# One head's masked scores added before the last matmul, an output tile and weights prepared in freed columns, and the second layer's input laid out by token block

## What is computed

```python
# layer 0: hx = rmsnorm(x) * (1 + scale) + shift
(k_f, lf_f), (k_b, lf_b), v = _hgrn2_gates(h, w_in, lb)
q, z = jnp.split(h @ w_in[:, 3 * HGRN_WIDTH:], 2, axis=-1)
# gla_forward, once forward and once on reversed tokens
o_inter = jnp.einsum('bhnck,bhnkv->bhncv', q_c * jnp.exp(b_c), s_prev)
a = jnp.einsum('bhnck,bhnsk->bhncs', q_c * jnp.exp(b_c - b_mid), k_c * jnp.exp(b_mid - b_c))
a = jnp.where(tril, a, 0.0)
o_intra = jnp.einsum('bhncs,bhnsv->bhncv', a, v_c)
# o = o_f + o_b, rmsnorm per head, times silu(z), times w_out, gated residual
# layer 1: x = x + gate * ((y.astype(h.dtype) * silu(z)) @ w_out), with
u, z = jnp.split(h @ w_in, 2, axis=-1)
pooled = centred means of u over windows 2, 4, 8, 16 of a 64-token row, minus u
y = jnp.einsum('brwgi,gio->brwgo', pooled, w_grp) * scale
# then a final rmsnorm
```

## Time and profile before

| what | value |
|---|---|
| three timed executions, median | 2196.77 us |
| lowest, highest | 2195.98, 2197.83 us |
| the profiled execution's own time | 2198.93 us |
| its span, first to last instruction | 2197.1 us |
| mean granted TensorE clock | 0.985 |
| busy: TensorE, VectorE, ScalarE, GpSimd | 96%, 58%, 42%, 22% |

### The profile page before, as it was taken

The page is one execution under the profiler, slowest core; times in us unless marked ns, Lnnn a source line. Parts: engine busy times, 40 slices in busy tenths (PEclk is TensorE's granted clock), DMA queues, the critical chain, the costliest instruction groups (busy, mean ns, idle before and its releaser), DMA issues.

```text
span 2197.1 us, 30841 instructions
## 1 busy us (share of the span) xinstructions
PE 2111.0 (96%) x11810; PEld 1526.6 (69%) x11810; DVE 1284.9 (58%) x2328; ACT 930.7 (42%) x1968; POOL 475.5 (22%) x441
## 2 busy tenths in 40 slices
PE   5899999999999999999999999899999999998998
PEld 2667767777777777777777777677666666665665
DVE  7847547547557547557457457655553536465444
ACT  5745345345355355355255355444423131214222
POOL 2021222222222322322313212000151312100110
PEclk8899999999999999999999999899999999999999
DMA  6210110110110110210110110534221110203443
GB/s 273 91 53 11 45 53 11 51 47 11 58 39 11 58 39 11 63 34 11 63 35 14 59 34 21 182 125 144 97 71 51 39 63 19 86 10 134 150 148 114
DMA packets 106746, 144.36 MB, mean 66 GB/s; under 512 B 7136, under 2 KB 74224, under 8 KB 105584
## 3 DMA queue, kind: packets, MB, share of 16 engines
q1 hardware_dynamic: 99648, 125.72, 17.6%
q10 hardware_dynamic: 6960, 16.80, 2.0%
HBM read 108.91 MB, written 33.57 MB: 65 GB/s over the span
## 4 chain that ended last, share of the span: by engine, by line
PE 83%; ACT 6%; DVE 6%; issue 2%; DMA 1%; SPq 0%; DVEq 0%; ACTq 0%
PE bank L1253 22%; PE bank L1254 22%; PE bank L1258 21%; PE bank L1408 3%; PE bank L1393 3%; PE bank L1388 3%; PE bank L1419 3%; PE bank L1508 3%; PE bank L1372 1%; DVE xa L1036 1%; ACT kp L713 1%; DMA ada_sb<-in_ada_w 1%; DVE lacc L1095 1%; ACT junk L385 1%; PE bank L1350 1%
## 5 line engine op out<-in xcount | busy, mean ns | idle before, releaser
L1253 PE MATMUL bank<-h_hi,w_hi 128*128 128x512 f32 (+1 forms) x1472 | 576.7, 397 | 0.0
L1254 PE MATMUL bank<-h_hi,w_lo 128*128 128x512 f32 (+1 forms) x1472 | 549.6, 378 | 0.0
L1258 PE MATMUL bank<-h_lo,w_bf 128*128 128x512 bf16 (+1 forms) x1472 | 328.6, 366 | 0.0
L1253 PEld LDWEIGHTS bank<-h_hi,w_hi 128*128 128x128 f32 x1472 | 278.9, 189 | 55.5
L1254 PEld LDWEIGHTS bank<-h_hi,w_lo 128*128 128x128 f32 x1472 | 279.1, 190 | 47.5
L1258 PEld LDWEIGHTS bank<-h_lo,w_bf 128*128 128x128 bf16 x1472 | 133.7, 98 | 142.7 <-issue 25.2
L1253 PE MATMUL bank<-wo_hi,og_hi 128*128 128x512 f32 x512 | 207.3, 405 | 11.9 <-DVE wo_lo L1128 7.8
L1066 DVE SCALAR_TENSOR_TENSOR w_st<-w_st,cv,bank 128x128 f32<-128x128 f32 x560 | 193.6, 346 | 30.0 <-PE bank L1408 6.2
L1254 PE MATMUL bank<-wo_hi,og_lo 128*128 128x512 f32 x512 | 202.2, 395 | 0.0
L578 POOL TENSOR_TENSOR q<-qp,cv 128x512 f32<-128x512 f32 x64 | 78.8, 1231 | 541.0 <-PE bank L1393 273.4
L553 POOL TENSOR_TENSOR w_hi<-w_raw,zero_col 128x512 fp32r<-128x512 f32 x80 | 91.9, 1149 | 425.9 <-PE bank L1258 224.3
(11 more groups left out here) (168 smaller groups left out, 3533.8 us busy)
## 6 DMA issues: line engine op xcount, KB each, us to landing
w_raw<-in_w_in SPq DMA_DIRECT2D x80, 256.0 KB, 2.7
ada_sb<-in_ada_w SPq DMA_DIRECT2D x8, 1024.0 KB, 13.7
xt<-in_x SPq DMA_DIRECT2D x16, 512.0 KB, 6.0
ada_a<-in_ada_late SPq DMA_DIRECT2D x64, 128.0 KB, 2.0
ada_b<-in_ada_late SPq DMA_DIRECT2D x64, 128.0 KB, 2.1
gated_scratch<-o_t ACTq DMA_DIRECT2D x32, 256.0 KB, 2.4
og<-gated_scratch SPq DMA_DIRECT2D x16, 512.0 KB, 4.1
xr<-in_x SPq DMA_DIRECT2D x16, 512.0 KB, 4.9
```

The lines of the kernel that those rows point to most:

```text
L1253: pe.matmul(out_ap, hi, m_hi, start=start, stop=False)
L1254: pe.matmul(out_ap, lo, m_hi, start=False, stop=False)
L1258: return pe.matmul(out_ap, bf, m_lo, start=False, stop=stop)
```

## The change

1. **Masked scores added.** The forward masked scores of all four blocks are kept; the backward ones go into one tile `am_b`. VectorE adds the two (`asum`, 128x512), in iterations 18 to 21 ahead of the chain, and TensorE multiplies `asum` with v once, in the backward iterations. The forward iterations keep only the product with the states. GpSimd clears one tile more.
2. **Late modulation.** Its buffers move into the columns of `k_tok`. In the first head its pieces come in iterations 5 to 9 (3, 3, 3, 3 and 4), and the closing matmuls in 9 and 10; in the other heads the pieces stay and the matmuls move from 8 and 12 to 7 and 10. Two copies of `k_tok` on ScalarE wait for them.
3. **First output tile.** It is loaded right after the output weights, into input columns that the heads have done with, rounded on ScalarE and VectorE within iteration 22 of the last head. GpSimd, not ScalarE, cuts the high parts of the eight weight slices. The wide part of the tile waits for high parts alone (`wo_cut`), the bf16 part for the rests. The last transpose of the heads follows the first tile's product.
4. **Layer 1's input by token blocks.** `h1_hi` and `h1_lo` get a block index ahead of the k index. The first projection of layer 1 comes before the transposes of the last tile.
5. **Group loop.** It is written out, and the first projection of a group waits like all others.
6. **Last weights.** The raw second half is loaded once block slot 0 has been used for the last time; slices 0 to 3 are rounded, and slices 0 and 1 get their rests, in iterations 14 and 15 of the last group, with the first tile.

```diff
-def late_index(st, first, top):
-
-    i = 2 * (st - (4 if first else 1)) - (1 if top else 0)
-    return i if 0 <= i < NLATE else None
+def late_pieces(st, first, top):
+
+    if first:
+        n = 4 if st == 9 else 3
+        seen = range(3 * (st - 5), 3 * (st - 5) + n) if 5 <= st <= 9 else range(0)
+        return seen[:1] if top else seen[1:]
+    i = 2 * (st - 1) - (1 if top else 0)
+    return range(i, i + 1) if 0 <= i < NLATE else range(0)
...
-    return {11: 0, 14: 1}.get(st) if first else {8: 0, 12: 1}.get(st)
+    return {9: 0, 10: 1}.get(st) if first else {7: 0, 10: 1}.get(st)
...
+                if g == 3 and n == NBLK:
+                    sp.wait_ge(s["proj_done"], HEADS * NG + 61)
+                    for j in range(2, 4):
+                        sp.dma_start(wo_raw1b[:, 2 * j - 4:2 * j - 2, :],
...
+            load_gated(sp, 0, 0)
             sp.wait_ge(s["x_done"], NX * HEADS)
-            load_gated(sp, 0, 0)
...
+            pool.wait_ge(s["proj_done"], HEADS * NG)
+            pool.wait_ge(s["gate_out"], 16)
+            for k in range(KT):
+                pool.wait_ge(s[f"wo_in{k // 2}"], 16)
+                pool.tensor_copy(wo_hi0[:, k, :], wo_raw0[:, k, :]).then_inc(s["wo_cut"], 1)
             round_gated(0)
...
+                    if last and st == NG - 1:
+                        round_tile(0, 0)
...
+                    if last and st == NG - 1:
+                        rest_tile(0, 0)
...
                     fi = st - (F0 + 3)
+                    if 6 <= fi < NF:
+                        ai = lat(fi)
+                        need(dve, "a_masked", NA, h, ai + 1)
+                        need(dve, "o_done", NA, h, ai)
+                        dve.tensor_tensor(asum[:, :, :], am[:, GROUPS[F0 + fi][1], :, :], am_b[:, :, :], ALU.add
+                                          ).then_inc(s["a_summed"], 1)
...
-            rest_weights(0, range(3))
-            rest_tile(0, 0)
-            rest_weights(0, range(3, KT))
+            rest_weights(0, range(KT))
+            rest_tile(0, 1)
             gate_out(HEADS, -1)
...
+                    if g == 3 and st == 14:
+                        rest_weights(1, range(1))
+                    if g == 3 and st == 15:
+                        rest_weights(1, range(1, 2))
+                        rest_tile(1, 0)
...
-                        need(pe, "a_masked", NA, h, ai + 1)
-                        for j in range(4):
-                            last = pe.matmul(o[:, j * P:(j + 1) * P], am[:, 2 * d + ai % 2, j, :],
-                                             v_tok[:, 2 + 4 * b + j, :], start=False, stop=True,
-                                             skip_group_check=True)
+                        if d == 1:
+                            need(pe, "a_summed", 4, h, ai - 3)
+                            for j in range(4):
+                                last = pe.matmul(o[:, j * P:(j + 1) * P], asum[:, j, :], v_tok[:, 2 + 4 * b + j, :],
+                                                 start=False, stop=True, skip_group_check=True)
                         last.then_inc(s["o_done"], 1)
...
+                pe.wait_ge(s["proj_read"], HEADS * NG + g * 16 + st - 1)
...
             for i in range(NTL + 1):
                 if i < NTL:
                     out_proj(0, i)
+                    if i == 0:
+                        turn_out(HEADS, -1)
+                else:
+                    pe.wait_ge(s["yg_ready"], 2 * (NTL - 1))
+                    pool_project(0, 0)
```

325 lines of the change are left out of this document (178 added, 147 removed).

## The result

| what | before | after |
|---|---|---|
| median of five timed executions | 2196.77 us | 2185.98 us |
| lowest, highest | 2195.97, 2197.83 | 2184.23, 2186.89 |
| the profiled execution's span | 2197.1 | 2183.6 |
| mean granted TensorE clock | 0.985 | 0.991 |

A forecast was written before the change was run, and what follows sets the result against it. TensorE, at 96% of the span, was taken as the bound, with VectorE setting the pace mid-head. Gains of 5.6, 1.5, 2.5, 6.9, 3.5 and 8.1 sum to 28.1 us, giving 2168.6, range 2158 to 2178.

The forecast's parts named there:

- Heads 2 to 8: Adding masked scores on VectorE shortens TensorE's list; 0.8 us gained per head, 5.6 us for seven heads.
- the slack of 1.66 in iteration 19 becomes 0.98, and the lead is cut to that: At line 1388: the sum of 0.68 ahead of VectorE's chain reduces its slack, limiting TensorE's lead to 0.98 us.
- The rule that spoke against it: VectorE's two-SBUF-input instructions contend with GpSimd's SBUF reads; a sum caught behind a cut would put the 5.6 near 0.
- First head: Late modulation pieces bring a 4.7 us wait in iteration 10, net loss 2.3; four blocks return 4.36; 1.5 us gained.
- Heads to output: Second output tile starts earlier, paced by VectorE's rests, GpSimd turns costing 3.1; 2.5 us gained after 1.0 for slow clock.
- Layer 0 to 1: Layer 1's first projection fills TensorE's wait of 5.50 before the last transposes; 6.9 us gained after 0.4 for late slices.
- group loop: The wait at each group's start in layer 1 goes; 3.5 us gained over three times.
- layer 1 to output: Two slices and the first tile done early; last output's second tile starts at 2017.8 instead of 2025.92, 8.1 us gained.
- The full payment: Rival: VectorE's loop has unseen room, so the heads give 32.6 us instead of 7.1; time 2143.1, chance 0.10.
- The sums set the pace: Rival: sums at the contended 1.53 lengthen VectorE's loop, heads lose 51.3 us; time 2227.1, chance 0.05.
- The unpaid seams: Rival: work moved to the seams arrives but its inputs come late; gain 14.0 us, time 2182.8, chance 0.13.
- the signs named for a wrong forecast: In the changed profile: a head shorter by 3 us or more, or a sum above 1 us in every row.

The follow-up runs named there:

- Runs 1: Changed kernel with the masked scores computed as before, four matmuls in all eight iterations and no sum on VectorE: 2180.89 us, ratio 0.9923.
- 2: Changed kernel with GpSimd's six cutting instructions of iteration 19 reduced to 4 of 128 columns in each part: 2172.71 us, ratio 0.9884.
- run 9: Changed kernel with GpSimd's first two half-slice cuts waiting for VectorE's sum, one each in iterations 19 and 20, beside the chain: 2174.15 us, ratio 0.9893.
- 12: Changed kernel with scores as before (no sum), cuts beside the chain after the addition of `o_t`, q slice's cuts after iteration 0's projection: 2181.11 us, ratio 0.9925.
- run 13: Kernel of run 11 with the first head's GpSimd cuts of iteration 9 waiting for the first product with k: 2167.92 us, ratio 0.9864.
- 14: Changed kernel with the first projection of layer 1 put back behind the last transposes of layer 0: 2191.31 us, ratio 0.9966.
- run 11: Changed kernel with cuts beside the chain, later q cuts, first head's iteration 9 pieces split two and two, second closing matmuls in 11: 2170.00 us, ratio 0.9875.

## Why the prediction was wrong

**Heads 2 to 8 (-5.6 forecast, +5.3 measured): the step that failed.** It is "the slack of 1.66 in iteration 19 becomes 0.98, and the lead is cut to that", and the 0.8 per head taken from it. Up to iteration 19 it holds: a lead of 1.0 is in the trace. But the reckoning stopped at the chain of iteration 18. It should have gone on to the chain of iteration 19, with two terms more: VectorE standing 1.64 later against TensorE, and its iteration 19 being 2.74 longer. The slack of 1.66 was spent twice: once as TensorE's lead, and once as distance between VectorE's start and GpSimd's. With it gone, GpSimd's work began 1.7 us earlier in VectorE's iteration, at its products. "The second sum of a head falls where GpSimd cuts weights" was seen, but as a price of this one sum; what grew was the whole iteration, by 2.74, of which the sum is 0.93. Runs 1, 2, 9 and 12 show it: no sum, no cuts, cuts elsewhere with and without the sum. Where no cut lies on the sums, adding the scores wins about what was forecast: heads of 162.0 against 162.86, 0.86 each where 0.8 was reckoned. So the lead and its cutting at the chain were right, and that VectorE's loop otherwise stays as long as it is was wrong.

**The rule that spoke against it.** In this case VectorE's products with two SBUF inputs took up to 1.78 beside GpSimd's cuts in place of 0.68, and the chain, which takes one large input from a PSUM bank, 3.12 either way. The Trainium skill (SBUF — State Buffer, "Who interferes with whom") says that instructions with two SBUF inputs contend with GpSimd's reads, and that those with at most one, outside VectorE's two-port modes, do not; the trace agrees with that. The prediction cited it for one sum per head, and gave it this term near 0. It should have been asked of every instruction that would come to lie beside a cut.

**First head (-1.5, +5.8).** The wait was forecast at 4.7 and is 5.79, since cuts lay on the pieces too (1.42, 1.07 and 1.06 in place of 0.45 to 0.48; run 13 moves them off). Then the term left out the clock behind the wait, 0.53 over 5 us, and counted four blocks at full payment where the heads had only 1.0 to give. That "this head had more slack at line 1388" was not worked out, and was wrong from iteration 19 on, where it loses the same 1.7 as the others. Of the 5.8, 4.7 had been lost by the first line 1446, where a net 2.3 was forecast.

**Heads to output (-2.5, -4.5).** The tile and its order were right; the rests paced the bf16 part, with five waits of 0.53. That the rests' end was nearly right is in part luck. They began at 1410.40, 10.3 behind the heads' last product where 7.4 was reckoned, since VectorE's work ahead of them was longer beside GpSimd's eight casts (the tile's rest took 2.05, a rest without casts beside it 1.21). But the casts were over at 1409.66, so none of the turns reckoned at 3.1 were taken, and the rests ended 19.4 behind the last product where 19.9 was reckoned. The 1.0 taken off for a slow clock was not due: TensorE was busy 17.13 of the 24 us from 1398 to 1422, its longest wait was 2.50, and the granted clock there was 1.00.

**Layer 0 to 1 (-6.9, -7.8), group loop (-3.5, -3.7), layer 1 to output (-8.1, -7.7).** These hold, in the sizes too. The slices came 0.52 late where 0.4 was taken off; the second tile came 13.6 after the last projection where 13 was forecast. Of these edits only the one to the first projection of layer 1 was undone in a run (14); the others are read from the two traces alone.

**The rivals.** None had this case. The full payment had the fact in hand, "GpSimd's cuts start earlier too, since they follow line 1393", and counted it as room on VectorE, where it was the loss. "The sums set the pace" asked whether a sum costs more than 0.58; it cost 0.68 to 0.93 and that was not what decided. The unpaid seams gave a time near the measured one, 2182.8, but for a reason that is absent. Nor would the signs named for a wrong forecast have caught this: no head is 3 us shorter, and no sum took 1 us.

Run 13 beats both kernels: 2167.92, a ratio of 0.9864 to the kernel before. It is also near the forecast of 2168.6. For heads 2 to 8 there is a reason: by the traces they take 5.2 us less than before the change, where 5.6 was forecast, once the cuts lie beside the chain. That the first head's 1.3 comes near its 1.5 is chance, since this head's pieces and cuts stand elsewhere than in the kernel that was forecast.

## What to carry to other kernels

A slack between two engines is often also the distance that keeps a third engine's work off the first: before spending it, look at who is released by the engine that gets faster, and what its instructions then lie on. Follow a lead through every iteration to the end of the period, not to where it is first cut. When cutting or casting on GpSimd is free to move, start it with the stretch in which VectorE takes one of its two inputs from PSUM; such a wait on a semaphore, with half of the cuts moved an iteration on, was worth 11 us here (run 9).

## What was not expected of the hardware

- Beside GpSimd's work VectorE's instructions that are not products took three to six times as long too: a copy of 128x8 took 0.62 to 1.05 in place of 0.17, and a `TENSOR_SCALAR` of 128x512 with one SBUF input 1.49 in place of 0.42 (run 11). The kernel before had it as well: the same `TENSOR_SCALAR` took 1.51 beside a cut, at 720.62. The Trainium skill (the same section) names copies and `tensor_scalar` among those that can enter a two-port mode, so the trace agrees with it; the prediction had looked at two-input instructions alone.
- `COPY_PREDICATED` from a bank (0.73 at 719.40 of the kernel before) and the addition of a bank to `o_t` (0.68 at 725.93 of the changed one) were as long beside cuts as without.
- GpSimd is held up as well: the same three cuts took 1.04, 1.15 and 1.73 beside VectorE's products and 1.04, 0.61 and 1.29 beside its chain.
- Moving an instruction of 0.68 us from ahead of a chain to behind it made the kernel 10.6 us slower. Earlier cuts, a granted clock of 0.62 behind a wait of 1.92, and the q slice's cuts on the last sum of a head all have a part in it; no run separates them.
